# Experts' results added to the output block by block through gather and store, in place of a table of block results combined at the end

## What is computed

```python
top_p, top_i = lax.top_k(jax.nn.softmax(e_logits, axis=-1), MOE_TOP_K)
top_w = g_gate[:, None] * top_p / jnp.sum(top_p, axis=-1, keepdims=True)
...
def expert_rows(args):
    xb, e = args
    hid = jax.nn.silu(xb @ w_gate[e]) * (xb @ w_up[e])
    return hid @ w_down[e]
y_rows = lax.map(expert_rows, (x_rows, block_expert)).reshape(n_rows, d)
y = jnp.zeros_like(xf).at[row_token].add(y_rows * row_weight[:, None].astype(y_rows.dtype))
...
h = h + hier_moe(u, ...)
```

## Time and profile before

| | |
|---|---|
| median of 3 runs | 1741.14 us (1739.82 to 1741.84) |
| span of the profiled execution | 1742.8 us |
| PE busy in the span | 1602.9 us (92%) |
| DVE, ACT, POOL busy | 1251.0, 640.8, 361.2 us |
| granted TensorE clock, mean | 0.963 |
| DMA | 292.62 MB, mean 168 GB/s |

### The profile page before, as it was taken

The page is one execution under the profiler, slowest core; times in us unless marked ns, Lnnn a source line. Parts: engine busy times, 40 slices in busy tenths (PEclk is TensorE's granted clock), DMA queues, the critical chain, the costliest instruction groups (busy, mean ns, idle before and its releaser), DMA issues. The chain is left out here.

```text
span 1742.8 us, 25255 instructions
## 1 busy us (share of the span) xinstructions
PE 1602.9 (92%) x7334; PEld 1257.3 (72%) x7334; DVE 1251.0 (72%) x2272; ACT 640.8 (37%) x1074; POOL 361.2 (21%) x495
## 2 busy tenths in 40 slices
PE   4999999999999999999998864999999999999991
PEld 3778888878878788888887753666776776677660
DVE  4567868768778588787785837776776777677754
ACT  4332333222322322323332321654554555455530
POOL 2122131131221311212212111122122212221210
PEclk9999999999999999999999965999999999999996
DMA  4122121121121211211213623799999999999927
GB/s 148 37 58 68 43 79 31 55 68 43 55 67 43 74 37 55 67 43 55 67 43 97 227 92 127 260 370 352 354 369 357 356 357 361 354 341 350 359 101 294
DMA packets 138508, 292.62 MB, mean 168 GB/s; under 512 B 17920, under 2 KB 68528, under 8 KB 137392
## 3 DMA queue, kind: packets, MB, share of 16 engines
q1 hardware_dynamic: 129056, 274.68, 45.1%
q0 software_dynamic: 9360, 16.80, 2.6%
HBM read 283.42 MB, written 25.30 MB: 177 GB/s over the span
## 5 line engine op out<-in xcount | busy, mean ns | idle before, releaser
L1658 ACT ACTIVATE gu_hi<-w_gu 128x1024 fp32r<-128x1024 f32 x256 | 272.7, 1066 | 311.6 <-PE g_ps L1701 233.3
L1755 DVE TENSOR_TENSOR gu_lo<-w_gu,gu_hi 128x1024 fp32r<-128x1024 f32 x256 | 313.5, 1226 | 90.1 <-ACT gu_hi L1658 66.9
L1005 PE MATMUL proj<-uTh,wl 128*128 128x512 f32 x768 | 310.7, 405 | 13.1 <-issue 6.6
L1007 PE MATMUL proj<-uTh,wh 128*128 128x512 f32 x768 | 302.4, 394 | 0.0
L1006 PE MATMUL proj<-uTl,wh 128*128 128x512 f32 x768 | 302.4, 394 | 0.0
L1719 PE MATMUL y<-w_d,hT 128*128 128x512 f32 x512 | 225.1, 592 | 1.0 <-DVE hT L1781 1.0
L438 POOL TENSOR_TENSOR wl<-raw,wh 128x512 fp32r<-128x512 f32 x96 | 128.6, 1358 | 396.4 <-ACT wh L495 396.4
L1005 PEld LDWEIGHTS proj<-uTh,wl 128*128 128x128 f32 x768 | 146.1, 190 | 44.0 <-issue 7.3
L1719 PEld LDWEIGHTS y<-w_d,hT 128*128 128x128 f32 x512 | 94.9, 190 | 108.4 <-issue 107.1
L1007 PEld LDWEIGHTS proj<-uTh,wh 128*128 128x128 f32 x768 | 146.0, 190 | 32.0
L1006 PEld LDWEIGHTS proj<-uTl,wh 128*128 128x128 f32 x768 | 146.4, 191 | 28.7
(11 more groups left out here) (243 smaller groups left out, 2809.4 us busy)
## 6 DMA issues: line engine op xcount, KB each, us to landing
w_gu<-in_moe_w_gate_dram SPq DMA_DIRECT2D x128, 512.0 KB, 8.3
w_gu<-in_moe_w_up_dram SPq DMA_DIRECT2D x128, 512.0 KB, 8.9
w_d<-in_moe_w_down_dram SPq DMA_DIRECT2D x128, 512.0 KB, 5.6
raw<-in_ssd_w_in_dram SPq DMA_DIRECT2D x96, 256.0 KB, 3.5
E<-acum_dram SPq DMA_DIRECT2D x64, 256.0 KB, 3.5
raw<-in_ssd_w_out_dram SPq DMA_DIRECT2D x32, 256.0 KB, 2.9
w_gu<-y_dram SPq DMA_DIRECT2D x8, 1024.0 KB, 9.8
hacc<-in_x_dram SPq DMA_DIRECT2D x8, 512.0 KB, 7.3
```

The costliest lines, as they stand in the source:

```text
L1005: nc.tensor.matmul(out, al, bh, start=start, stop=False)
L1007: return nc.tensor.matmul(out, ah, bh, start=False, stop=stop)
L1658: nc.scalar.activation(wh[:, j % RING, :], weights.gate_up(b, j), ACT.Copy).then_inc(w_hi, 1)
L1755: vec.tensor_tensor(wl[:, j % RING, :], weights.gate_up(b, j), wh[:, j % RING, :].bitcast(F32), ALU.subtract).then_inc(w_lo, 1)
```

## The change

The residual is stored to the output first, in `routing` (eight stores ahead of the down weights on SP's queue). In `experts` every block fetches the rows of the output that belong to its tokens (`fetch`, an indirect DMA from `out` into `yb`), adds its result times the row's weight to them (`y_out`, now a multiply-add with `yb` as an input), and stores them back to the output (`scatter`). As two blocks may hold the same token, the fetch of block n waits until the scatter of block n-1 has landed. The table's second plane now carries the weight of each row (`wrow`) in place of a row number, `ridx` keeps only tokens, and `wtok`, `y_dram`, `y2` and the combine are gone. PE's instructions are the same.

```diff
@@ routing, block.sync
             sp.dma_start(biasb[:, EG:NL], b_expert.partition_broadcast(P)).then_inc(loaded, 16)
+            ov = out.rearrange("(i p) d -> p i d", p=P)
+            for i in range(NT):
+                sp.dma_start(ov[:, i, :], hacc[:, i, :]).then_inc(out_stored, 16)
             for b in range(2):
                 for j in range(8, NPC):
                     weights.load(sp, b, b, j)
@@ routing, block.gpsimd
             g.memset(zero[:], 0).then_inc(const_steps, 1)
-            pool.wait_ge(const_steps, 14)
+            g.memset(yb[:], 0.0).then_inc(const_steps, 1)
+            pool.wait_ge(const_steps, 15)
@@ routing, block.vector
-            link(vec.tensor_tensor(wtok[:, 0, :], s8[:, 3, :], s8[:, 10, :], ALU.mult))
-            link(vec.tensor_tensor(wtok[:, 1, :], wtok[:, 0, :], s8[:, 7, :], ALU.mult))
+            link(vec.tensor_tensor(src[:, 0, :, 1], s8[:, 3, :], s8[:, 10, :], ALU.mult))
+            link(vec.tensor_tensor(src[:, 1, :, 1], src[:, 0, :, 1], s8[:, 7, :], ALU.mult))
 
             for k in range(2):
                 link(vec.tensor_scalar(src[:, k, :, 0], toki[:], -PADROW, None, ALU.add))
-                link(vec.tensor_scalar(src[:, k, :, 1], toki[:], 2.0, k - PADROW, ALU.mult, ALU.add))
@@
-            link(vec.tensor_scalar(ridx[:], tab_ps[:], PADROW, None, ALU.add))
+            link(vec.tensor_scalar(ridx[:], tab_ps[:, 0, :], PADROW, None, ALU.add))
+            link(vec.tensor_copy(wrow[:], tab_ps[:, 1, :]))
@@ experts, block.sync
             load_down(last, 1)
 
-            for b in range(2):
-                sp.wait_ge(scattered[b], val(last, 0, 8, 16))
-            yv = y_dram.rearrange("(i p c) d -> p i c d", p=P, c=2)
-            ov = out.rearrange("(i p) d -> p i d", p=P)
-            for i in range(NT + 3):
-                if i < NT:
-                    if i >= 4:
-                        sp.wait_ge(comb, 2 * (i - 3))
-                    sp.dma_start(y2[i % 4], yv[:, i]).then_inc(y2_loaded[i % 4], 16)
-                if i >= 3:
-                    sp.wait_ge(comb, 2 * (i - 2))
-                    sp.dma_start(ov[:, i - 3, :], hacc[:, i - 3, :]).then_inc(out_stored, 16)
-            sp.wait_ge(out_stored, 16 * NT)
@@ experts, block.gpsimd
-            def scatter(p, b):
-
-                wait(pool, scattered[b], p, 0, 8, 0)
-                g.tensor_copy(stmp[:, b, :], ridx[:, 1, bass.ds(val(p, b, 1, 0), 1)]).then_inc(sidx_done, 1)
+            def fetch(p, b):
+
+                if b == 1:
+                    wait(pool, scattered[0], p, 0, 8, 16)
+                else:
+                    wait(pool, scattered[1], p, 0, 8, 0)
+                g.tensor_copy(stmp[:, b, :], ridx[:, bass.ds(val(p, b, 1, 0), 1)]).then_inc(sidx_done, 1)
                 wait(pool, sidx_done, p, b, 3, 1)
-                wait(pool, y_done, p, b, 2, 2)
                 g.tensor_tensor(sidx[:, b, :], stmp[:, b, :], zero[:], ALU.add).then_inc(sidx_done, 1)
                 wait(pool, sidx_done, p, b, 3, 2)
                 g.tensor_tensor(held[:, 1, :], zero[:], zero[:], ALU.add).then_inc(sidx_done, 1)
-                g.indirect_dma_start(y_dram, bass.IndirectOffsetOnAxis(sidx[:, b, :].bitcast(U32), 0), yb[:, b, :], None,
-                                     bounds_check=last_row, oob_is_err=False).then_inc(scattered[b], 16)
+                g.indirect_dma_start(yb[:, b, :], None, out, bass.IndirectOffsetOnAxis(sidx[:, b, :].bitcast(U32), 0),
+                                     bounds_check=last_token, oob_is_err=False).then_inc(fetched[b], 16)
+
+            def scatter(p, b):
+
+                wait(pool, y_done, p, b, 2, 2)
+                g.tensor_tensor(held[:, 2, :], zero[:], zero[:], ALU.add).then_inc(held_done, 1)
+                g.indirect_dma_start(out, bass.IndirectOffsetOnAxis(sidx[:, b, :].bitcast(U32), 0), yb[:, b, :], None,
+                                     bounds_check=last_token, oob_is_err=False).then_inc(scattered[b], 16)
@@ body
                     elif p[0] is not None or p[1]:
                         scatter(shifted(p, -1), 1)
+                    fetch(p, b)
 
             for ahead in range(3):
                 gather(FIRST, 0, ahead)
+            pool.wait_ge(out_stored, 16 * NT)
             last = pairs(pool, body, peeled=2)
             scatter(last, 1)
 
             pool.wait_ge(gathered[0], val(last, 0, 8, 32))
+            for b in range(2):
+                pool.wait_ge(scattered[b], val(last, 0, 8, 16))
@@ experts, block.vector
             def y_out(p, b):
-                wait(dve, scattered[b], p, 0, 8, 0)
+                wait(dve, fetched[b], p, 0, 8, 16)
                 for j in range(2):
                     wait(dve, y_mm, p, b, 2, j + 1)
-                    vec.tensor_copy(yb[:, b, j * 512:(j + 1) * 512], y_ps[j][:]).then_inc(y_done, 1)
+                    rows = yb[:, b, j * 512:(j + 1) * 512]
+                    vec.scalar_tensor_tensor(rows, y_ps[j][:], wrow[:, bass.ds(val(p, b, 1, 0), 1)], rows,
+                                             ALU.mult, ALU.add).then_inc(y_done, 1)
@@
-            for i in range(NT):
-                dve.wait_ge(y2_loaded[i % 4], 16 * (i // 4 + 1))
-                for c in range(2):
-                    if c:
-                        dve.wait_ge(comb, 2 * i + 1)
-                    vec.scalar_tensor_tensor(hacc[:, i, :], y2[i % 4][:, c, :], wtok[:, c, i:i + 1], hacc[:, i, :],
-                                             ALU.mult, ALU.add).then_inc(comb, 1)
```

More of the change, by code:

```diff
@@ L1191, in _, with routing @@
                 logits(k)
-def routing(nc, lg, ridx, etab, npairs, wtok, weights, xg, zero, ident, b_group, b_expert):
+def routing(nc, hacc, lg, ridx, wrow, etab, npairs, weights, xg, yb, zero, ident, b_group, b_expert, out, out_stored):
     NT = lg.shape[1]
@@ L1452, in _, with experts @@
             dve.wait_ge(tab_mm, 2 * NT)
-            link(vec.tensor_scalar(ridx[:], tab_ps[:], PADROW, None, ALU.add))
-def experts(nc, hacc, ridx, etab, npairs, wtok, weights, xg, zero, ident, u2_dram, y_dram, out):
+            link(vec.tensor_scalar(ridx[:], tab_ps[:, 0, :], PADROW, None, ALU.add))
+            link(vec.tensor_copy(wrow[:], tab_ps[:, 1, :]))
+def experts(nc, T, ridx, wrow, etab, npairs, weights, xg, yb, zero, ident, u2_dram, out, out_stored):
     _, D, FF = weights.src[0].shape
@@ L1464, in experts @@
     KF = FF // P
-    NT = hacc.shape[1]
-    T = NT * P
+    NT = T // P
     RING = 4
@@ L1484, in experts @@
         hT = sb("hT", [P, 2, KF, P])
-        yb = sb("yb", [P, 2, D])
         gidx = sb("gidx", [P, 2, 1], I32)
@@ L1489, in experts @@
         stmp = sb("stmp", [P, 2, 1], I32)
-        held = sb("held", [P, 2, 1], I32)
+        held = sb("held", [P, 3, 1], I32)
         tp = [psum(f"tp3_{j}", [P, 4, P]) for j in range(2)]
@@ L1495, in experts @@
         y_ps = [psum(f"y3_{j}", [P, 512]) for j in range(2)]
-        y2 = [weights.gu[j // 2][:].rearrange("p a k f -> p (a k f)")[:, (j % 2) * 2 * D:(j % 2 + 1) * 2 * D]
-              .rearrange("p (c d) -> p c d", c=2) for j in range(4)]
         w_hi = sem("w_hi3")
@@ L1505, in experts @@
         sidx_done = sem("sidx_done")
+        held_done = sem("held_done")
         gathered = [sem(f"gathered{b}") for b in range(2)]
+        fetched = [sem(f"fetched{b}") for b in range(2)]
         scattered = [sem(f"scattered{b}") for b in range(2)]
@@ L1516, in experts @@
         y_done = sem("y_done3")
-        y2_loaded = [sem(f"y2_loaded{j}") for j in range(4)]
-        comb = sem("comb")
-        out_stored = sem("out_stored")
         def val(p, b, per, add):
@@ L1597, in _ @@
             g = nc.gpsimd
-            last_token, last_row = pool.to_reg(T - 1), pool.to_reg(2 * T - 1)
+            last_token = pool.to_reg(T - 1)
             def gather(p, b, ahead):
@@ L1605, in gather @@
                 wait(pool, turned, p, b, 2, 2 * (ahead - 1))
-                g.tensor_copy(gtmp[:, par, :], ridx[:, 0, bass.ds(val(p, b, 1, ahead), 1)]).then_inc(gidx_done, 1)
+                g.tensor_copy(gtmp[:, par, :], ridx[:, bass.ds(val(p, b, 1, ahead), 1)]).then_inc(gidx_done, 1)
                 wait(pool, gidx_done, p, b, 3, 3 * ahead + 1)
@@ L1800, in layer @@
         hacc = ctx.enter_context(nc.sbuf_tensor("hacc", [P, T // P, D], F32))
-        ridx = ctx.enter_context(nc.sbuf_tensor("ridx", [P, 2, MAXB], I32))
+        ridx = ctx.enter_context(nc.sbuf_tensor("ridx", [P, MAXB], I32))
+        wrow = ctx.enter_context(nc.sbuf_tensor("wrow", [P, MAXB], F32))
         etab = ctx.enter_context(nc.sbuf_tensor("etab", [P, MAXB], I32))
         npairs = ctx.enter_context(nc.sbuf_tensor("npairs", [P, 3], I32))
-        wtok = ctx.enter_context(nc.sbuf_tensor("wtok", [P, 2, T // P], F32))
         acum_dram = nc.dram_tensor("acum_dram", [GROUPS * R * (T // P), P], F32).ap()
         u2_dram = nc.dram_tensor("u2_dram", [T, D], F32).ap()
-        y_dram = nc.dram_tensor("y_dram", [2 * T, D], F32).ap()
```

(7 more changed lines are left out.)

## The result

| | before | after |
|---|---|---|
| median | 1740.48 us (1738.56 to 1741.84) | 1731.73 us (1726.82 to 1733.27, 4 runs) |
| ratio after / before | | 0.9934 [0.9918, 0.9951] |
| profiled span | 1742.8 us | 1731.5 us |

The change gains 0.66% where 1.7% was forecast: 1731.73 against 1710.9 us. The forecast was 1707 to 1713 us, and the time lies well outside it. It lies within the stated range of 1707 to 1734 us only because that range took in the first rival, near the upper end of whose 1713 to 1734 it falls.

What follows compares the result with a forecast made beforehand. The prediction took PE to bound the expert part, with the DMA engines close behind. It summed -32.2 (end) + 0 (start) + 2 (middle) = -30.2 us, giving 1710.9 us; forecast 1707 to 1713, range 1707 to 1734.

Steps and rivals of the forecast that it cites:

- the first rival: In the blocks, the fetch-add-scatter loop is a little longer than PE's period: losses of 4 to 25 us, 1713 to 1734; chance 0.26.
- The end, removed: After the last scatter, the combine's loads, additions and stores go; a chain through the last two blocks replaces them: 32.2 us earlier.
- Before, 0.4 us lay between the last landing and the end of the span; I keep that: At the program's end, the span would close 0.4 us after the last scatter's landing at 1710.2, at 1710.6.
- The start: In routing, eight added 512 KB stores on SP's queue ahead of the down weights cost 0, with 1 us either way.
- The middle: In the blocks, the added wait closes a loop that must fit one 19.15 us period; 2 us allowed over all blocks.
- the free lateness of 3.1 us: In each block, y may start 3.1 us late at no cost to PE: 1.7 us DVE idle plus 1.4 us split margin.
- Landing of the fetch: a gather of the same size and shape ... lands in 6.4 us median: In the block loop, the fetch was taken to land like the earlier kernel's gathers: 6.4 us median, 5.3 to 7.7.
- 2.3 is under 3.1: In the blocks, y's lateness settles at 2.3 us, under the 3.1 us that costs PE nothing: no cost on medians.
- the end of the train absorbs the difference: DVE's train of weight splits ends at 1173.6 whatever happens, so y's lateness stops growing, at 2.3 us.
- The rate as a bound: Rival: DMA engines move at most 359 GB/s, so a block's 7.07 MB takes 19.7 us; 17 us lost, time 1726; chance 0.07.
- Slower than before: Rival: the block loop is 20.3 us or more, eating the whole gain at DVE's wait before the y additions; chance 0.10.
- profile after: Signs if right: gate/up period 19.15 us, last landing within 2 us of 1710; if wrong: PE idle behind splits, period 19.6 or more.

## Why the prediction was right, and where it was not

- **The end, removed.** The work that goes and the chain that takes its place were right: with the drain moved and nothing else, the last gate/up to the end takes 34.2 us, where 65.6 - 32.2 = 33.4 was forecast. The step that failed is "Before, 0.4 us lay between the last landing and the end of the span; I keep that". What ended the span before was SP's last store; once that is gone the last thing is POOL's drain, 8.0 us, which had been hidden under the combine at the earlier trace rows and did not show among the groups. That accounts for about 8 of the 8.6 us; the rest lies in a y of block 31 that begins 28.4 us behind the last gate/up and not 27.8. The landing of the last fetch, 4.2 us, was a guess between two bounds and hit by luck.
- **The start** was right: no cost (1.6 us the other way, less than the spread of the starts). The DMA share of routing's window rose from 0.32 to 0.59. SP's eight stores took 7.95 us to issue and not 4.8, with nobody waiting.
- **The middle.** That the loop exists, its order, POOL's operations (1.9 us from landing to issue, the first at 1.1 us beside the splits, where the forecast's last turn had 2.3) and the scatter's landing (8.3) were right. So was the free lateness of 3.1 us: the profiles of all kernels put it at 3.2. The step that failed is one term: "Landing of the fetch: a gather of the same size and shape ... lands in 6.4 us median". It measured 7.4. The term came from gathers of a kernel without the fetch's traffic, and this traffic is shown to slow the gathers; that it accounts for the fetch's own 1.0 us is likely, not shown. With it the loop is 1.85 + 8.3 + 2.0 + 7.4 = 19.6 us in place of 18.6, the one side of 19.15 and not the other. The prediction's own fixed point, "2.3 is under 3.1", had 0.8 us to spare against a term that was 1.0 short. That "the end of the train absorbs the difference" no longer helps there. The eight splits then run back to back and end 11.3 us behind the start of y (1212.21 against 1200.91), where they ended 14.5 behind it in the earlier trace rows. From then on their end moves with y, and POOL's first operation stays beside them. The prediction's first rival priced just this: 31 x 0.5 - 3.1 = 12.4 us; 13.9 were measured. It was given a chance of 0.26.
- **The rate as a bound** is refuted: all of the change's traffic fits in PE's period, at 373 and 377 GB/s over two windows of 100 us. The Trainium skill (DMA: Bandwidth & Descriptors, Specifications) states about 358 GB/s for a core; this core, alone at work, went past it. The Trainium skill (Perfetto Trace Analysis, Roofline) says that 358 is the share when both cores of a pair are active and that one alone can pull more, and these windows agree.
- **Slower than before** was the right mechanism with the point a little off. The forecast put it at a loop of 20.3 us, from a gain of 32 us at the end. With the 23.6 us that the end really gave, 31x - 3.1 = 23.6 gives x = 0.86, a loop of 20.0; the kernel with the longer loop, at 20.6, is on the far side.
- The "profile after" that the prediction named did its work: a period of 19.6 and PE waiting on splits meant the loop. Its bound of "less than 1 us of PE waiting on splits per block" could not tell: 13.9 us over 31 blocks are 0.45 each. It set 8 us as the landing at which the forecast falls; 7.2, which the text itself gave a few lines above, was the true edge.

Left open: why a transfer of 0.26 MB more in each block makes the gathers land 1.1 us later. That it comes with the fetch's traffic is shown; where in the engines or queues it waits is not. That moving the gather ahead of the fetch does not quicken the fetch is shown, but no run has a fetch in the loop that lands in 6.4 us.

## What to carry to other kernels

When a change adds a wait that closes a loop through the engines, sum the loop and set it against the period; if the margin is smaller than what the change's own traffic may add to a landing, take the loop as the bound. Then look first for what can be done before the wait: two small operations moved ahead of it were worth 12 us here. How late a result may come before anything waits is worth working out by itself: here it was right to 0.1 us, and what failed was a landing taken from a kernel with less traffic. When the end of a program is cut off, look for what had been running beside it, sequencer instructions at the last source line too, since these stand in no list of busy time.

## What the runs showed that was not expected

- POOL's drain grows with the indirect transfers since the last one: 5.5 us after 65 transfers, 8.0 after 97, 7.7 behind the last issue after 94, and 0.3 after the three behind an early drain. That is about (7995 - 5476) / 32 = 79 ns for each. All are of one size, so whether it is the transfers or their packets that count is not shown. It does not wait for the data: it runs on 5.8 us after the last landing. It costs nothing where POOL is idle.
- POOL's issue takes longer beside the splits. POOL's issue of the fetch took 1.04 us in the change and 1.9 to 2.1 us in 14 of 25 blocks of the kernel with early row numbers, each time with a split of DVE begun just before it. So these blocks gave back at POOL's issue, and not in the transfer, the microsecond that the early row numbers had taken out of the loop, and in sum it was still enough.
